# First product-key layer computed densely for both token tiles, with the first tile's chain behind it

## The chip, the core and the metric

The kernel runs on one core of one Trainium2 chip. The metric is device time in microseconds (us), from the start of the program on the core to its end. All arithmetic that matters here is float32. The engines are named as in the profile: PE is TensorE (matmuls), PEld its weight loads, DVE is VectorE, ACT is ScalarE, POOL is GpSimd (which here issues the gathers), SP is SyncE (which here issues all other loads).

## The reference, cut to what matters

One batch of 256 tokens with 1,024 features passes through a first block (token mixing, attention, 32 experts) and then a second block of two layers. The change touches the feed-forward part of the second block's first layer, a product-key memory:

```python
def peer_ffn(h, w_q, sub_keys, u_tab, v_tab):       # T = 256 tokens, D = 1024
    q = (xt @ w_q).reshape(T, PEER_HEADS, 2, PEER_HALF)         # 8 heads
    s = jnp.einsum('thpd,hpnd->thpn', q, sub_keys)              # 2 x 128 key scores
    sv, si = lax.top_k(s, PEER_TOPK)                            # 16 of 128
    cand = sv[:, :, 0, :, None] + sv[:, :, 1, None, :]
    cv, ci = lax.top_k(cand.reshape(T, 8, 256), PEER_TOPK)      # 16 of 256 pairs
    ...
    eidx = (i1 * PEER_NKEYS + i2)                               # row of 16,384
    gates = jax.nn.softmax(cv, axis=-1)
    uc = jnp.take(u_tab, ic, axis=0); vc = jnp.take(v_tab, ic, axis=0)
    act = jax.nn.gelu(jnp.einsum('cd,ckd->ck', xc, uc))
    return jnp.einsum('ck,ckd->cd', gc * act, vc)
```

A token uses 8 x 16 = 128 of the 16,384 rows of `u_tab` and of `v_tab` (64 MiB each). After it follow a gated embedding, and then in the second layer keys and values, stick-breaking attention, and a second product-key memory with tables of its own.

## The kernel before

The tokens are two tiles of 128. Up to the recurrent part everything is dense. Then come four phases of 128 steps, `f` = 0 to 3 (`PHASES`): phases 0 and 1 are the first memory for tile 0 and tile 1, phases 2 and 3 the second memory for tile 0 and tile 1. A step `k` handles one pick of each of the 128 tokens:

- POOL gathers 128 rows of 8 KiB (key and value side by side, `uv0` or `uv1`) into one of 10, later 13, row buffers: 1 MiB a step.
- DVE (`share`, line 2170) multiplies each row by its token and sums; ACT takes the gelu (1664 or 1662) of a pair of steps; DVE multiplies by the gate (2199 or 2196); ACT spreads each coefficient on a diagonal (1669).
- PE (`picks`, 1245) multiplies the diagonal by the value rows and adds into two banks: two matmuls of 512 columns a step.

A phase has 64 ticks of two steps. In a tick `t` of phase `f` >= 1, a piece of `chain(f - 1, t)` is issued behind the picks on each engine. `chain(q)` is all that follows a memory for a tile: `chain(0)` and `chain(1)` are the embedding of the first layer, keys, values, queries, attention in four groups of heads, output product, and the queries and scores of the second memory; `chain(2)` and `chain(3)` are only the last embedding and norm. So `chain(0)` runs under phase 1, `chain(1)` under phase 2.

The choice of rows is DVE's: a unit is one head of one tile (`UNITS` = 16 in a layer), cut in four pieces, `best_keys` twice, `best_pairs`, `rows_of` (lines 2104 to 2150). A list of ticks (`FIRST_CHOICES`, `chosen`) sets where a piece stands between the shares. A gather waits for the unit's numbers (`idx_ready`) and for a free row buffer (`rows_used`, counted by PE).

The weights of a chain, 60 chunks of 512 KiB, are loaded by SP into a ring of 6 slots in the order in which the chain uses them; earlier loads use a ring of 8. SP waits for a slot's last use (`w_used`) before it refills it.

Of the kernel before, what the change touches and what calls it, by code (L numbers as in the profile page):

```python
# [31 lines left out]
P = 128  # L32
T = 256
# [29 lines left out]
ROWS, MORE_ROWS, MORE_AT = 10, 3, 170  # L63
ROW = 2 * D
UNITS = TT * PH
# [24 lines left out]
FIRST_NEXT, ASK_HERE, ASK_NEXT = 0, 11, 19  # L90
FIRST_CHOICES = {0: (1, 2), 1: (1, 3), 2: (2, 0), 4: (2, 1), 6: (2, 2), 8: (2, 3), 10: (3, 0), 12: (3, 1), 14: (3, 2),
# [3 lines left out]
QUERY_GROUPS = (range(0, 4), range(4, 8))  # L95
EARLY = 10
PLE_EARLY = 5

# [35 lines left out]
def plan():  # L134

    first, n = {}, 0
    for name, chunks in (
        ("w_in", 16), ("w_pool", 1), ("w_out", 8), ("w_router", 1), ("b_down", 1), ("proj0", 2), ("ple0", 8),
        ("a_x", 8), ("a_y", 8),
        ("wqa", 8), ("wqb", 8),  # L140
        *((f"{name}{q}", chunks) for q in range(TT) for name, chunks in (
            ("proj_", 2), ("ple_", 8), ("kv", 16 - EARLY * (q == 0)), ("bq", 8), ("bo", 8),
# [15 lines left out]

def row_buffer(k):

    return k % ROWS if k < MORE_AT else (k - MORE_AT + ROWS) % (ROWS + MORE_ROWS)


ROW_COUNT = []
for _k in range(PHASES * PHASE):
    ROW_COUNT.append(sum(row_buffer(m) == row_buffer(_k) for m in range(_k + 1)))


def chosen(f, t):

    if f == 0:
        return [FIRST_CHOICES[t]] if t in FIRST_CHOICES else []
    now = [(PH * f + 2 + j // 4, j % 4) for j in range(24) if int(1.75 * j) == t]
    if f < PHASES - 1 and CHOOSE <= t < CHOOSE + 8:
        now.append((PH * (f + 1) + (t - CHOOSE) // 4, (t - CHOOSE) % 4))
    return now


def by_tanh(f, t):

    return 1 <= f <= TT and t // SHARES in TANH_UNITS
# [29 lines left out]
def program(nc, io, out):  # L211
    first = plan()
    slot, slot_loads, freed_by = ring_plan(first)
    with ExitStack() as ctx:
# [36 lines left out]
        def half(bank, e):  # L251
# [19 lines left out]
            "pq_ready scores_kept tok_ready idx_ready cv_ready cv_exp dots_ready gelu_ready coef_ready "  # L271
            "diags_ready rows_used x_turned x_kept xk_ready rms_kept hs_ready h_turned hd_act hd_dve gate_kept "
            "k_copied k_turned k2_ready v2_ready q_copied q_turned q2_ready "
            "z_done ln_ready spm_ready rc_done arg_ready w_exp a_ready o_done o_ready tile_done scored sq_tile ss_tile rt_tile gates_done sums_in sq_summed root_turned col_ready early_used late_used "
            "out_ready out_stored moe_step gu_used dn_used"
# [3 lines left out]
        keys_loaded, gates_loaded = sem("keys_loaded"), sem("gates_loaded")  # L279
        early_loaded, late_loaded = sem("early_loaded"), sem("late_loaded")  # L280
# [65 lines left out]
        early = [at(k * D, D) for k in (0, 1, 2, 3, 6, 7, 8, 9, 10, 11)]  # L346
# [6 lines left out]
        sums_bank = (7, 6, 4, 6, 0, 1, 7, 4)  # L353
# [12 lines left out]
        def asked(z, tt):  # L366

            return scr if z else (big[:, 5 * ROW:5 * ROW + D], mT[:, D:2 * D])[tt]

        def ask_bank(z, tt):  # L370

            return ((4, 4), (4, 0))[z][tt]

        def score_bank(z, tt):

            return ((0, 4), (4, 0))[z][tt]
# [14 lines left out]
        diag_at = small[:, 2304:2304 + DIAGS * P]  # L391

# [54 lines left out]
        def _(sync):  # L447
# [107 lines left out]
            for z in range(2):  # L555
                sync.dma_start(keys0[z], io["sub_keys"][0][:, z * SLOT:(z + 1) * SLOT]).then_inc(keys_loaded, 16)
            for k in range(EARLY):
                c, z = k % DT, k // DT
                sync.dma_start(early[k], io["w_kv"][c * P:(c + 1) * P, z * SLOT:(z + 1) * SLOT]).then_inc(early_loaded, 16)
            dense("wqa", io["peer_w_q"][0], 2)  # L560

            def ple_chain(q):
                if q == 0:
                    sync.wait_ge(w_used, first["proj0"] + 2)
# [1846 lines left out]
```

## Time and profile before

| what | us |
|---|---|
| measured, median of 3 runs (lowest, highest) | 2735.54 (2732.45, 2740.74) |
| profiled execution, span from first to last instruction | 2730.7 |
| PE busy | 2497.4 |
| DVE busy | 1372.8 |
| ACT busy | 626.5 |
| POOL busy | 494.7 |
| bytes moved | 1058.03 MB, mean 387 GB/s |

The profile gives no time of its own for the profiled execution beyond this span; the median of the runs is 4.8 us above it, which is what lies around the span. Busy PE time is the union of pipelined matmuls, so for groups of matmuls of one kind the busy time divided by their count is the interval from one to the next. An "x8" row of the timeline is eight instructions merged.

### The profile page before, as it was taken

Reading aid. Unit: us, or ns where it says so; the run is one execution under the profiler, and the core shown is the slowest. Engines: PE = TensorE matmul, PEld = TensorE weight load, DVE = VectorE, ACT = ScalarE, POOL = GpSimd, SP = SyncE. Lnnn points to the kernel's source line nnn. Section 1 sums busy time; section 2 is a strip of 40 time slices with the busy share of each in tenths; the row PEclk is TensorE's granted clock in tenths of the full one; section 3 lists DMA queues with packets and bytes.
Section 4 is the critical chain, followed back from the end, with each engine's and each line's share of the span. In section 5 each row is a group of like instructions: output and inputs, shape, how many; then the busy total and the mean of one; then the engine's idle time right before and its main releaser. Section 6 shows DMA issues by size and latency. Waiting matters only on the chain.

```text
span 2730.7 us, 30447 instructions
## 1 busy us (share of the span) xinstructions
PE 2497.4 (91%) x10712; PEld 1284.3 (47%) x10712; DVE 1372.8 (50%) x3805; ACT 626.5 (23%) x1464; POOL 494.7 (18%) x534
## 2 busy tenths in 40 slices
PE   8899999999999999997987889989799899788786
PEld 6744444444444444995643334436344446333332
DVE  2411222222212222757677776785675775678753
ACT  0300110100100001232322342332332432332212
POOL 1000000000000000003333333332332332333330
PEclk9989999999999999998999999999999999999999
DMA  7689999999999997549999999999999999999993
GB/s 250 262 325 409 429 428 429 428 428 428 428 429 427 430 427 296 183 170 381 421 420 421 421 419 383 419 420 418 420 418 417 420 418 417 417 411 421 421 421 165
DMA packets 135686, 1058.03 MB, mean 387 GB/s; under 512 B 15744, under 2 KB 16168, under 8 KB 45472
## 3 DMA queue, kind: packets, MB, share of 16 engines
q0 software_dynamic: 75104, 540.07, 47.9%
q1 hardware_dynamic: 60480, 516.70, 45.8%
q8 instruction: 52, 0.85, 0.1%
q14 instruction: 50, 0.41, 0.0%
HBM read 1055.64 MB, written 2.63 MB: 388 GB/s over the span
## 4 chain that ended last, share of the span: by engine, by line
PE 55%; DMA 28%; DVE 12%; ACT 3%; issue 2%; SPq 0%; DVEq 0%; POOL 0%; POOLq 0%
PE ps L773 15%; PE ps L1245 15%; DMA big<-in_uv,small 14%; DMA big<-in_w_gate_up 13%; PE ps L763 4%; PE ps L927 4%; DVE big L2170 4%; PE ps L1042 2%; PE ps L1198 2%; PE ps L1058 2%; PE ps L809 1%; PE ps L623 1%; PE ps L695 1%; DMA ring<-in_uv,small 1%; PE ps L1005 1%
## 5 line engine op out<-in xcount | busy, mean ns | idle before, releaser
L1245 PE MATMUL ps<-big,small 128*128 128x512 f32 x1940 | 922.5, 622 | 171.1 <-ACT small L1669 170.9
L2342 POOL DMA_INDIRECT big<-in_uv,small x485 | 458.9, 946 | 2086.6 <-DVE small L2150 1182.7
L773 PE MATMUL ps<-big 128*64 128x512 f32 x3072 | 701.7, 601 | 11.6 <-DMA big<-in_w_gate_up 7.7
L2170 DVE SCALAR_TENSOR_TENSOR big<-big,ps 128x1024 f32<-128x1024 f32 x485 | 580.8, 1217 | 213.9 <-DMA big<-in_uv,small 213.6
L1245 PEld LDWEIGHTS ps<-big,small 128*128 128x128 f32 x1940 | 371.7, 199 | 662.1 <-issue 410.7
L773 PEld LDWEIGHTS ps<-big 128*64 128x64 f32 x3072 | 205.5, 137 | 397.7 <-issue 355.4
L1669 ACT ACTIVATE small<-con,small 128x128 f32<-128x128 f32 x512 | 177.6, 394 | 322.4 <-DVE small L2199 273.2
L1908 DVE COPY big<-ps 128x512 f32<-128x512 f32 x32 | 22.1, 692 | 417.5 <-PE ps L773 417.5
L1894 DVE TENSOR_TENSOR big<-ps,big 128x256 f32<-128x256 f32 x64 | 27.2, 425 | 284.7 <-PE ps L791 284.7
L1664 ACT ACTIVATE small<-small 128x2 f32<-128x2 f32 x224 | 45.7, 204 | 495.1 <-DVE big L2170 479.1
L927 PEld LDWEIGHTS ps<-hT,ring 128*128 128x128 f32 x1152 | 134.5, 194 | 14.7 <-issue 10.5
L927 PE MATMUL ps<-hT,ring 128*128 128x128 f32 x1152 | 135.6, 278 | 3.7 <-DVE hT L1968 3.7
L763 PEld LDWEIGHTS ps<-small,mT 128*128 128x128 f32 x1024 | 120.0, 196 | 26.6 <-issue 26.6
L763 PE MATMUL ps<-small,mT 128*128 128x64 f32 x1024 | 124.4, 281 | 1.3 <-DVE small L1876 1.3
L1421 ACT COPY big<-ps 128x512 f32<-128x512 f32 x32 | 18.7, 585 | 412.9 <-PE ps L773 412.9
L2199 DVE SCALAR_TENSOR_TENSOR small<-small 128x2 f32<-128x2 f32 x224 | 49.2, 220 | 124.3 <-ACT small L1664 122.8
L1413 ACT ACTIVATE big<-big 128x256 f32<-128x256 f32 x64 | 26.6, 416 | 218.2 <-DVE big L1895 218.2
L1042 PE MATMUL ps<-ring,xT 128*128 128x512 f32 x152 | 68.3, 593 | 0.0
L1245 PE MATMUL ps<-ring,small 128*128 128x512 f32 x108 | 54.9, 634 | 13.0 <-ACT small L1669 13.0
L809 PE MATMUL ps<-small,big 64*128 64x256 f32 x512 | 63.9, 390 | 0.0
L1198 PEld LDWEIGHTS ps<-xT,ring 128*128 128x128 f32 x512 | 59.5, 192 | 6.7 <-issue 6.7
L1401 ACT COPY big<-ps 128x512 f32<-128x512 f32 x32 | 18.7, 586 | 184.3 <-PE ps L773 184.3
(338 smaller groups left out, 2104.8 us busy)
## 6 DMA issues: line engine op xcount, KB each, us to landing
big<-in_w_gate_up SPq DMA_DIRECT2D x128, 2048.0 KB, 21.0
big<-in_w_down SPq DMA_DIRECT2D x64, 2048.0 KB, 22.4
ring<-in_peer_w_q SPq DMA_DIRECT2D x48, 512.0 KB, 10.7
ring<-in_ple_w_gate SPq DMA_DIRECT2D x22, 512.0 KB, 10.5
ring<-in_w_kv SPq DMA_DIRECT2D x22, 512.0 KB, 10.4
ring<-in_w_in SPq DMA_DIRECT2D x16, 512.0 KB, 7.1
ring<-in_a_w_in SPq DMA_DIRECT2D x16, 512.0 KB, 4.7
ring<-in_b_w_q SPq DMA_DIRECT2D x16, 512.0 KB, 11.7
```

Source lines behind the costliest of these rows:

```text
L763: last = pe.matmul(ps[:, G_X, c * CAP:(c + 1) * CAP], mT[:, tt * D + c * P:tt * D + (c + 1) * P], m_sel[:, tt * CAP:(tt + 1) * CAP], start ...
L773: last = pe.matmul(ps[side * CAP:(side + 1) * CAP, bank + b, :], o, w[:, at:at + BANK], start=start, stop=stop, skip_group_check=True)
L809: last = pe.matmul(half(G_OUT, side * DT // 2 + c), m_y[at, c * P:(c + 1) * P], m_gateT[at, :], start=False, stop=True, skip_group_check=True)
L927: last = pe.matmul(ps[:, bank + e // 4, (e % 4) * P:(e % 4 + 1) * P], w[:, e * P:(e + 1) * P], src(c)[:, tt * P:(tt + 1) * P], start=(c == ...
L1042: last = pe.matmul(ps[:, bank + z, :], src[:, blocks(c)], w[:, z * BANK:(z + 1) * BANK], start=(c == 0), stop=(c == DT - 1), skip_group_ch ...
L1058: last = pe.matmul(ps[:, bank + half_, :], src[:, blocks(c)], w[:, half_ * BANK:(half_ + 1) * BANK], start=(c == 0), stop=(c == DT - 1), s ...
L1198: last = pe.matmul(ps[:, A + e // 4, blocks(e % 4)], w[:, blocks(e)], hd[:, blocks(c)], start=(c == 0 and e % 4 == 0), stop=(c == DT - 1), ...
L1245: last = pe.matmul(ps[:, out_bank(f) + z, :], diagonal(k), rows(k)[:, D + z * BANK:D + (z + 1) * BANK], start=(k % PHASE == 0), stop=((k + ...
L1669: act.activation(diagonal(k), ident, ACT.Copy, scale=coef[:, k % PICKS:k % PICKS + 1])\
L2170: ins = dve.scalar_tensor_tensor(r, r, 1.0, tok, op0=ALU.mult, op1=ALU.mult, accum_out=dots[:, k % PICKS:k % PICKS + 1])
L2199: dve.scalar_tensor_tensor(coef[:, at], acts[:, at], p_rec[:, u16:u16 + 1], cv[:, at], op0=ALU.mult, op1=ALU.mult).then_inc(S["coef_ready" ...
L2342: pool.indirect_dma_start(out=rows(k), out_offset=None, in_=io[f"uv{n // UNITS}"], in_offset=bass.IndirectOffsetOnAxis(ap=rows_at[:, at:at ...
```

## The change

Phases 0 and 1 are replaced. Instead of gathering the chosen rows, the kernel streams all of both tables once, and computes every key's score for every token of both tiles:

- `key_block`: for each of 128 blocks (one second-key number, 128 first-key numbers) one chunk of 512 KiB is loaded into the ring of 8 and multiplied by all 256 tokens: 8 matmuls of 256 columns. `keep_keys` on ACT takes the gelu of two blocks at a time into `weighed`, 128 KiB per partition that cover all of `big`.
- `choose`: all 16 units are chosen without shares between them; the row number is not formed, the two key numbers and the scores are kept. `gates` makes the softmax weights, `turn_picks` transposes numbers and gates to have a token's 128 picks on the partitions.
- `place`, 64 times: for 8 tokens and 64 second keys, DVE builds one-hot rows of the first keys (`hot`, 1,024 wide) and gate-weighted one-hot rows of the second keys (two operations of 512), PE multiplies them token by token (8 matmuls of 64 columns, the sum over a token's 128 picks), and DVE multiplies `weighed` by the outcome (`weigh`, 512 wide, from PSUM). 32 of them stand between the later key blocks, 32 between the first 63 value blocks.
- `value_block`: for each of 128 blocks a chunk of 512 KiB is multiplied by `weighed`: 4 matmuls of 512 columns, two tiles by two halves.
- `chain(0)` is issued alone after the last value block, then phase 2 with `chain(1)` and phase 3 with `chain(2)` as before. The second memory's gathers begin with unit 16, which is chosen at ticks 51 to 54 of that lone chain; all 13 row buffers are free by then. The ten early key and value weights of `chain(0)` are now loaded by the ring; the second half of the first queries' weights takes their place.

```diff
+            def key_block(k):
+                w, bank = chunk(first["u"] + k), KEY_BANK + k // 2 % 2
+                if k % 2 == 0 and k >= 4:
+                    pe.wait_ge(S["keys_kept"], k - 2)
+                for c in range(DT):
+                    done = pe.matmul(ps[:, bank, k % 2 * T:(k % 2 + 1) * T], w[:, c * P:(c + 1) * P], tile(hT, c), ...)
+                done.then_inc(w_used, 1)
+            def place(b):
+                tt, t0, tokens, lo, n = placing(b)
+                pe.wait_ge(S["hot_ready"], b + 2)
+                if b == 32:
+                    pe.wait_ge(S["keys_kept"], BLOCKS)
+                if b >= 2:
+                    pe.wait_ge(S["w_ready"], b - 1)
+                for j in range(tokens):
+                    done = pe.matmul(..., hot1[b % 2][:, j * P:(j + 1) * P], hot2[b % 2][:, j * n:(j + 1) * n], ...)
+                done.then_inc(S["placed"], 1)
+            def value_block(k):
+                if k in PLACED_BY:
+                    pe.wait_ge(S["w_ready"], PLACED_BY[k])
+                w = chunk(first["v"] + k)
+                for tt in range(TT):
+                    for z in range(2):
+                        done = pe.matmul(ps[:, out_bank(tt) + z, :], weighed[tt][:, k * P:(k + 1) * P], w[:, z * BANK:(z + 1) * BANK], ...)
+                done.then_inc(w_used, 1)
+            pe.wait_ge(S["idx_ready"], PH // 2)
+            for k in range(BLOCKS):
+                key_block(k)
...
+            for k in range(BLOCKS):
+                value_block(k)
...
+            for t in range(TICKS):
+                chain(0, t)
-            for f in range(1, PHASES):
+            for f in range(TT, PHASES):
...
+            def keep_keys(j):
+                used_through(act, "u", 2 * j + 2)
+                for tt in range(TT):
+                    act.activation(at, sums[:, :, tt * P:(tt + 1) * P], ACT.Gelu_apprx_tanh).then_inc(S["keys_kept"], 1)
+            for j in range(BLOCKS // 2):
+                keep_keys(j)
+                if j in EXPS_AT:
+                    exps(EXPS_AT[j])
...
+            def hot(b):
+                dve.tensor_tensor(one, iota..., of(0)..., ALU.is_equal)
+                link(dve.tensor_tensor(two, iota[:, lo:lo + n]..., of(1)..., ALU.is_equal))
+                dve.tensor_tensor(two, two, of(2)..., ALU.mult).then_inc(S["hot_ready"], 1)
+            def weigh(b):
+                dve.wait_ge(S["placed"], b + 2)
+                dve.wait_ge(S["keys_kept"], lo + n)
+                dve.tensor_tensor(w, ps[:, PLACE_BANK[b // 32] + b % 2, :].rearrange("p (t i) -> p i t", t=tokens), w, ALU.mult)
+            for b in range(PLACINGS):
+                weigh(b)
+                if b + 2 < PLACINGS:
+                    hot(b + 2)
-            for n in range(2 * UNITS):
+            for n in range(UNITS, 2 * UNITS):
                 pool.wait_ge(S["idx_ready"], n + 1)
```

`EXPS_AT` puts the exponentials of unit `n` behind key pair `5 * (n - 3) // 2 + 1`, `PICKS_AT` puts `turn_picks` behind pair 36, and `PLACE_IN_KEYS` spreads 32 placings over pairs 37 to 62.

Three places in the order of instructions. PE, from the end of the recurrent output product, before (L927 is `one_tile`, here the queries of tile 1, and L1245 the picks):

```order
L1005 MATMUL ps<-mT,big 128x128 x24
L1227 MATMUL ps<-con,hT 128x128 x8
L942 MATMUL ps<-small,con 128x128
L927 MATMUL ps<-hT,ring 128x128 x8
L1245 MATMUL ps<-big,small 128x512 x4
...
L1245 MATMUL ps<-big,small 128x512 x8
L1219 MATMUL ps<-big,mT 128x128 x8
```

And now (L1252 is `second_queries`, L1269 `key_block`, L1278 `turn_picks`, L1290 `place`):

```order
L1026 MATMUL ps<-mT,big 128x128 x24
L1252 MATMUL ps<-hT,big 128x128 x32
L963 MATMUL ps<-small,con 128x128
...
L1234 MATMUL ps<-big,mT 128x128 x8
L1269 MATMUL ps<-hT,ring 128x256 x16
L1234 MATMUL ps<-big 128x128 x8
L1269 MATMUL ps<-hT,ring 128x256 x576
L1278 MATMUL ps<-con,small 128x128 x6
L1269 MATMUL ps<-hT,ring 128x256 x16
L1290 MATMUL ps<-small,mT 128x64 x16
```

The queries that stood between picks are now issued in one piece, and 74 key blocks (16 + 576 matmuls, 8 a block) stand before `turn_picks`; from there one or two placings stand behind each pair of blocks.

PE in `chain(0)`, at its gate and keys, before (L1058 is keys and values, L1065 a transposition):

```order
L1058 MATMUL ps<-ring,xT 128x512 x4
L1245 MATMUL ps<-big,small 128x512 x4
L1042 MATMUL ps<-ring,xT 128x512 x4
L1245 MATMUL ps<-big,small 128x512 x4
L1042 MATMUL ps<-ring,xT 128x512 x4
```

And the same chain now, from the last value blocks (L1301) on (L1063 is L1042 of before, L1073 is L1058, L1080 is L1065, L1165 the attention scores):

```order
L1301 MATMUL ps<-ring,big 128x512 x260
L1099 MATMUL ps<-ring,pT 128x512 x4
L1080 MATMUL ps<-con,big 128x128 x8
L1063 MATMUL ps<-ring,xT 128x512 x16
L1080 MATMUL ps<-con,big 128x128 x8
L1073 MATMUL ps<-ring,xT 128x512 x24
L1080 MATMUL ps<-con,big 128x128 x8
L1073 MATMUL ps<-ring,xT 128x512 x8
L1063 MATMUL ps<-ring,xT 128x512 x16
L1080 MATMUL ps<-con,big 128x128 x8
L1165 MATMUL ps<-xT,big 128x128 x4
```

The picks between the chain's pieces are gone; nothing else stands between them. DVE, from the last unit of the first memory to the first placings, now (L2222 ends `rows_of`, L2384 and L2386 are `gates`, L2390 takes the turned picks, L2400 to L2404 are `hot`, L2412 is `weigh`):

```order
L2222 TENSOR_REDUCE small<-small 128x16
L2384 RECIPROCAL small<-small 128x16
L2386 TENSOR_TENSOR small<-small 128x256
L2390 COPY small<-ps 128x3x128 x2
L2400 TENSOR_TENSOR mT<-con,small 128x1024
L2402 TENSOR_TENSOR small<-con,small 128x512
L2404 TENSOR_TENSOR small<-small 128x512
L2400 TENSOR_TENSOR mT<-con,small 128x1024
L2402 TENSOR_TENSOR small<-con,small 128x512
L2404 TENSOR_TENSOR small<-small 128x512
L2412 TENSOR_TENSOR big<-ps,big 128x64x8
```

Before, a pair of `share` operations of 1,024 elements stood between any two pieces of a unit; now units 2 to 15 follow each other directly behind the norm of the second tile, and the placings come after the last of them.

## Rows read from the trace of the kernel before

**Rows 1.** The page: span, busy us of each engine, GB/s in 40 slices.
```profile
span 2730.7 us, 30447 instructions
PE 2497.4 (91%) x10712; PEld 1284.3 (47%) x10712; DVE 1372.8 (50%) x3805; ACT 626.5 (23%) x1464; POOL 494.7 (18%) x534
...
GB/s 250 262 325 409 429 428 429 428 428 428 428 429 427 430 427 296 183 170 381 421 420 421 421 419 383 419 420 418 420 418 417 420 418 417 417 411 421 421 421 165
```

**Rows 2.** Phases: stretch, PE PEld DVE ACT POOL busy (count), PEclk, DMA share, GB/s.
```profile
1244.00:1586.00 342.00, 297.18 (x968) 155.43 (x968) 250.33 (x676) 91.13 (x243) 120.53 (x128) 0.93 1.01 420
1586.00:1984.00 398.00, 358.30 (x1112) 176.68 (x1112) 275.70 (x760) 132.41 (x311) 127.34 (x134) 0.98 1.01 413
1984.00:2387.00 403.00, 361.61 (x1186) 183.27 (x1185) 267.98 (x728) 131.75 (x297) 119.86 (x127) 0.97 1.02 418
2387.00:2700.00 313.00, 256.04 (x553) 104.34 (x552) 220.28 (x553) 83.66 (x225) 107.61 (x114) 0.96 0.97 403
```

**Rows 3.** Who waited for whom, 1244 to 2700: us, times, longest.
```profile
DVE big L2170 <- DMA big<-in_uv,small: 213.6, 169, 3.5
```

**Rows 4.** Timeline, PE: start, duration, instructions of one kind in a row.
```profile
19.93 20.99 PE L623 MATMUL ps<-hT,ring 128*128 128x256 f32 x96
...
1211.64 9.20 PE L1257 MATMUL ps<-hT,ring 128*128 128x128 f32 x80
...
1705.44 3.60 PE L1042 MATMUL ps<-ring,xT 128*128 128x512 f32 x8
```

**Rows 5.** Timeline, DVE: the first unit's pieces, and the first share.
```profile
1221.77 0.30 DVE L2104 MAX8 small<-ps 128x8 f32<-128x128 f32 x1 [8.35 <-PE ps L1267]
...
1225.21 0.18 DVE L2126 CAST small<-small 128x32 f32<-128x32 uint32 x1
...
1228.20 0.17 DVE L2140 TENSOR_SCALAR small<-small 128x16 uint32<-128x16 uint32 x1
...
1231.77 0.17 DVE L2148 SCALAR_TENSOR_TENSOR small<-small 128x16 f32<-128x16 f32 x1
...
1243.79 1.22 DVE L2170 SCALAR_TENSOR_TENSOR big<-big,ps 128x1024 f32<-128x1024 f32 x1
```

**Rows 6.** Groups by line and shape: busy, mean ns of one, idle before.
```profile
L1957 DVE TENSOR_REDUCE small<-mT 128x128 f32<-128x1024 f32 x4 | 7.6, 1912 | 1.4 <-ACT mT L1459 1.4
L2249 DVE TENSOR_TENSOR big<-ps,big 128x512 f32<-128x512 f32 x8 | 5.5, 685 | 10.6 <-ACT big L1551 10.6
```

**Rows 7.** Bytes by queue, 1984 to 2700.
```profile
q0 software_dynamic: 35611, 259.28, 87.3%
q1 hardware_dynamic: 9792, 34.87, 12.2%
```

**Rows 8.** Timeline, the last rows and the last chain, engines together.
```profile
2699.19 1.22 DVE L2170 SCALAR_TENSOR_TENSOR big<-big,ps 128x1024 f32<-128x1024 f32 x1 [1.23 <-DMA big<-in_uv,small]
...
2705.21 1.29 DVE L2215 TENSOR_TENSOR hT<-ps,hT 128x512 f32<-128x512 f32 x2 [4.30 <-PE ps L1245]
...
2708.70 1.07 ACT L1528 ACTIVATE big<-hT 128x1024 f32<-128x1024 f32 x1
...
2711.17 0.29 ACT L1529 ACTIVATE small<-small,eps 128x1 f32<-128x1 f32 x1
```

**Rows 9.** Timeline, ACT: the logarithm of a group of heads in `chain(0)`.
```profile
1742.41 1.28 ACT L1601 ACT_TABLE_LOAD   x1
1743.70 0.63 ACT L1601 ACTIVATE big<-big 128x512 f32<-128x512 f32 x1
```

**Rows 10.** Loads of 512 KiB: median us to landing; busy and GB/s at 60:100.
```profile
ring<-in_w_out SPq DMA_DIRECT2D x8, 512.0 KB, 3.8
...
big<-in_w_kv SPq DMA_DIRECT2D x10, 512.0 KB, 11.7
...
60.00:100.00 40.00, 37.64 (x183) 27.02 (x182) 17.76 (x58) 17.23 (x52) 0.00 (x0) 1.00 0.86 349
```

**Rows 11.** Busy and clock where PE resumes after waiting.
```profile
1244.00:1248.00 4.00, 3.72 (x16) 3.42 (x16) 3.90 (x12) 0.20 (x1) 0.69 (x1) 0.50 1.02 426
```

More of the change, by code:

```diff
@@ L570, in _ @@
[L570 to L582 removed]
+                sync.dma_start(keys0[z], io["sub_keys"][0][:, z * SLOT:(z + 1) * SLOT]).then_inc(gates_loaded, 16)
@@ L583, in _ @@
+            for t in range(TICKS):
+                chain_weights(0, t)
+            for t in range(TICKS):
+                chain_weights(1, t)
             sync.wait_ge(w_used, first["proj_1"] + 2)
@@ L1236, in residual, with second_queries @@
                 for c in range(DT):
-                    last = pe.transpose(ps[:, 4 + c // 4, (c % 4) * P:(c % 4 + 1) * P],
-                                        tile(xT, c)[:, tt * P:(tt + 1) * P], ident)
-                last.then_inc(S["x_turned"], 1)
+                    done = pe.transpose(narrow(TURN_BANK, c), tile(xT, c)[:, tt * P:(tt + 1) * P], ident)
+                done.then_inc(S["x_turned"], 1)
+            def second_queries(tt, between=()):
+                pe.wait_ge(early_loaded, 16 * DT)
+                for c in range(DT):
+                    for e in range(DT):
+                        done = pe.matmul(narrow(ask_bank(1, tt), e), wqb[c][:, e * P:(e + 1) * P],
+                                         tile(hT, c)[:, tt * P:(tt + 1) * P], start=(c == 0 and e % 4 == 0),
+                                         stop=(c == DT - 1), skip_group_check=True)
+                    if tt:
+                        done.then_inc(S["early_used"], 1)
+                    elif c == DT - 1:
+                        done.then_inc(S["tile_done"], 1)
+                    for after, piece in between:
+                        if c == after:
+                            piece()
@@ new lines, in key_block @@
+            def key_block(k):
+                w, bank = chunk(first["u"] + k), KEY_BANK + k // 2 % 2
+                if k % 2 == 0 and k >= 4:
+                    pe.wait_ge(S["keys_kept"], k - 2)
+                for c in range(DT):
+                    done = pe.matmul(ps[:, bank, k % 2 * T:(k % 2 + 1) * T], w[:, c * P:(c + 1) * P], tile(hT, c),
+                                     start=(c == 0 and k % 2 == 0), stop=(c == DT - 1), skip_group_check=True)
+                done.then_inc(w_used, 1)
@@ new lines, in _ @@
+            pe.wait_ge(S["idx_ready"], PH // 2)
+            for k in range(BLOCKS):
+                key_block(k)
+                if k == 1:
+                    scores(1, 1)
+                if k % 2:
+                    if k // 2 == PICKS_AT:
+                        turn_picks()
+                    for b in PLACE_IN_KEYS[k // 2]:
+                        place(b)
+            for k in range(BLOCKS):
+                value_block(k)
+                if k in RESIDUAL_AT:
+                    residual(RESIDUAL_AT[k])
+                if k in PLACE_IN_VALUES:
+                    place(PLACE_IN_VALUES[k])
```

356 lines of the change are left out of this document (191 added, 165 removed), and 3 rows, old and new, of the table FIRST_CHOICES.

## The prediction

> **What bounds the kernel now.** I read the busy time by stage first. From 1244 to 2700 us, the four phases, the 16 DMA engines are busy 97 to 102% of the time and move 403 to 420 GB/s, whatever else goes on [rows 2]. PE is busy 82 to 90% there, DVE 66 to 73%. The page alone would mislead: over the span PE has the larger share, 91% [rows 1], but its records overlap and part of that busy time is at a lower granted clock (0.93 in phase 0). The waits decide it: the dot products on DVE waited 213.6 us in 169 pieces for gathered rows [rows 3], and those rows could not come faster. So phases 0 to 3 last as long as their bytes: 1.05 MB a step, 134.2 MB a phase, plus the chain's weights. Phases 0 and 1 take 1984 - 1244 = 740 us [rows 2], and they hold the whole of `chain(0)` as free cover for PE, ACT and DVE.
>
> **The change, part by part.** I follow absolute times in the profiled execution, up to the last share's first gather, then add what comes behind.
>
> *Start of the key blocks.* PE's first key block waits for four finished units. A unit is on DVE from 1221.77 to 1231.77 plus two short operations [rows 5]: keys 3.4 us, pairs 3.0, rows 3.6 without these two, which fall away: 10.0 us. At 1243.8 the second tile's norm is done and unit 1 has its keys [rows 5]. Left are 6.6 us of unit 1 and units 2 and 3, 20 us: the blocks start at 1270.4. PE has 128 + 64 query matmuls of 128 columns until then, 0.115 us each (9.20/80) [rows 4], 22 us, so it waits for DVE, not DVE for it.
>
> *Key blocks.* 1,024 matmuls of 256 columns. An unbroken run of such matmuls takes 20.99 us for 96, less the pipe's end of 0.35: 0.215 us each [rows 4]. That is 220.2 us. The load of a block is 0.524 MB in 1.72 us, 305 GB/s, below what the queue shows (next paragraph but one). DVE must meanwhile finish units 4 to 15: 12 x 10.0 = 120 us, and PE reaches `turn_picks` after 37 pairs, 127 us. ACT's exponential of unit 15 stands behind pair 31 (at 111 us) and its pair scores come at 116; ACT then holds back the gelus, and PE, two banks ahead, loses 1 to 2 us.
>
> *Placings.* 512 matmuls of 64 columns. No such matmul stands alone before; I take the interval of a 128-column one, 0.11 us, since its weights are as wide: 57 us for all 64 placings, on PE and not hidden. As DVE work a placing costs 1.2 us (1,024 elements, as the share's 1.22 [rows 5]) and three times 0.69 (512 elements [rows 6]), with overlap 3.2 us. PE offers one per 3.69 us during keys (26 x 3.44 / 32 + 0.9) and one per 4.4 during values, so DVE fits. First wait: two `hot` of 2.6 us after the picks are turned, about 2 us beyond a pair.
> The price of `weigh` is the open one: it reads PSUM and walks `weighed` with strides. A reduction that reads 1,024 strided elements takes 1.91 us [rows 6], 1.87 ns an element against 1.34 for the plain 512. Bounds: 0.69 us, or 0.96, and as a far end twice that, 1.9. At 0.96 a placing is 3.5 us and still fits. At 1.9 it is 4.4, PE waits 0.7 us in each of 32 placings in the keys and none in the values: +22 us. I take nothing.
> The Trainium skill (SBUF — State Buffer, "Door 1: The DMA port swizzle") says that each access that crosses to a new 16-byte line pays a penalty, and that any non-contiguous PSUM pattern significantly slows matmuls. The strided reduction agrees in direction (1.91 us); no row here shows a strided PSUM read, and if it tripled `weigh` the 22 us above would be due.
>
> *Value blocks.* 512 matmuls of 512 columns at 0.429 us (3.60/8 with 0.17 of pipe end [rows 4]): 219.7 us. The transposes of picks and residual are 22 small ones, 2.5 us. I add 8 us: ACT 1.5, first placing 2, and PE's wait before the blocks and after the turn, since PE comes back at a granted clock of 0.50, 1.2 GHz, after waiting [rows 11].
> End of the values: 1270.4 + 220.2 + 57.3 + 219.7 + 2.5 + 8 = 1778.
>
> *Are the loads hidden?* 134.2 MB in 508 us are 264 GB/s, 305 at the peak. 512 KiB loads: ten in a row landed after 11.7 us in the median, and with larger ones between, 349 GB/s were moved while PE was the one that asked [rows 10]. Alone such a load lands in 3.8 us [rows 10]; eight in flight would be 8 x 0.524 / 3.8 = 1,100 GB/s, more than the engines have. So the ring of 8 hides them.
> The Trainium skill (DMA: Bandwidth & Descriptors, "Measured (HBM→SBUF, 128 partitions, SWDGE, issued from GpSimd)") asks for at least 1 MiB a DMA for 75% of peak; by it the change halves the size to where less is had. Its table is for one DMA at a time. The case of 349 GB/s above is against it.
>
> *`chain(0)` alone.* Before, it had 398 us of cover; now each step counts. From rows of the last chain [rows 8]: add 1.3, turn and gains 2.3, square to root 2708.70 to 2711.46 = 2.8, reciprocal and scale 0.9. Steps to the embedding's gate 7.5; its 16 matmuls 7.3; sigmoid with table load and the two products 4.1; square, scale, turn, eight gains 7.2; keys and values 32 x 0.43 = 13.7, but ten of their chunks come at 1.25 us (0.524 MB at 420 GB/s [rows 2]), so 16; the queries likewise 8 x 1.25 = 10; copy, turn, keep 4. Four groups of heads: from ln to ln a group passes DVE twice 0.69, PE sums and the next scores 1.5, abs, exp, exp and ln at 0.63 each [rows 9] and some 0.7 of handing over, 6.1 us; a table load of 1.28 on the first [rows 9], and 12 us for the first half of the first and the second half of the last: 30. Merge 5.6, add to gains 7.5, first queries 7.2 and their copy, scores and keep 3.6, unit 16 10.3. Sum 120. PE waits often here, so part of its 65 us of matmuls (84 of 512 columns at 0.43, 128 of 128 at 0.115, some 14 us of transposes, scores and attention) runs at 1.2 GHz as in [rows 11]; I take 10 us for it (bounds: 0, and 65 if all of it). First gather: 1778 + 130 = 1908.
>
> *Phases 2 and 3.* They stay bound by bytes. From 1984 to 2700 SP's queue moved 34.9 MB [rows 7], the same work as now. The gathers are all 256: 268.4 MB instead of the 259.3 counted there, since none can be ahead of the lone chain. 303.3 MB at phase 2's 418 GB/s [rows 2] are 725.6 us; 1.5 for the first to arrive. Behind the last row, 2699.2 to 2730.7, are 31.5 us [rows 1, 8]. End: 1908 + 1.5 + 725.6 + 31.5 = 2667 us, 64 less than the span of 2730.7. The median of the runs lies 4.8 above that span: 2672.
>
> In bytes: 268 MB of gathers for the first layer become 134 MB of streams, which saves 320 us of DMA; about 260 of them are given back, since PE's 497 us of new matmuls and 130 us of chain have no bytes beneath them.
>
> **The rivals.**
> A. *The lone chain is slower than summed* (half clock nearly throughout, loads later, handing over dearer): its bound of 65 us instead of 10 adds 55, end at 2727. For it: PE resumed at 0.50 [rows 11] and attention has many waits. Against: gate, keys to queries, and merge to scores are runs of 7 us and more. With half of it, 2700.
> B. *DVE sets the pace of the placings*: +22 us in the keys, 2694; if `hot` with its broadcasts is also dearer, by a third (+1 us), +32 more in keys and +32 in values, 2758. For it: no row has this broadcast at this width. Against: the share of 1,024 elements takes 1.22 us with one operand in PSUM [rows 5], so the width alone costs nothing more.
> C. *The streams are bound by DMA: slower than before.* At the 250 GB/s of the span's first slice [rows 1], whose loads are of this size, 134.2 MB take 537 us instead of 508, +29: 2701. It decides from 134.2 MB / (508 + 64) = 235 GB/s down; at the 170 of the weakest slice before the phases [rows 1], 789 us and 2953. Against: 349 GB/s [rows 10], and that those slices stand where PE does not ask for more.
> D. *The chain is quicker and PE never waits*: 120 for the chain, 3 instead of 8: 2657.
> That the change doesn't do what it says I leave out: the order of PE shows both streams and the lone chain.
>
> **How the numbers follow.** Forecast with D's side, 2650 to 2692: 0.62. A, 2692 to 2727: 0.18. B: 0.12, of which 0.03 above 2744. C: 0.05, of which 0.03 slower. Faster still, below 2650: 0.03. A measurement of this kernel tells 0.3%, 8.2 us: same is 2727 to 2744. Faster 0.89, same 0.05, slower 0.06. The range leaves out a tenth or less at each end: 2648 to 2716.
>
> **What would show it.** Right: PE busy near 100% from 1270 to 1778 at clock 1.00, matmuls of 256 columns at 0.215 us and of 512 at 0.43, DMA near 270 GB/s; PE waiting for DVE before the first key block; the first gather 125 to 135 us after the last value block; then 418 GB/s for 725 us. Wrong: PE waiting for `in_u_blocks` or `in_v_blocks` (C), for the products on L2404 or L2412 with DVE near 100% (B), a chain of 160 us or more (A), or a second memory that starts below 418 GB/s, because DVE chooses unit 17 before its first share while 13 buffers fill.

## The result, and the profile after

| | us, median | lowest to highest |
|---|---|---|
| before | 2735.2 (4 runs) | 2732.45 to 2740.74 |
| after | 3229.03 (4 runs) | 3227.3 to 3231.69 |

The changed kernel is 18% slower: ratio 1.181, 95% interval 1.1793 to 1.1827. The forecast said 2672 us. The profiled execution has a span of 3227.1 us; by the forecast's own sum it should have been 2667.

The page of the changed kernel, against [rows 1]: the busy time of each engine, GB/s in 40 slices, and the engines of the chain that ended last.

```profile
span 3227.1 us, 35837 instructions
PE 3033.2 (94%) x13774; PEld 1789.1 (55%) x13774; DVE 1235.1 (38%) x3327; ACT 548.3 (17%) x1202; POOL 253.8 (8%) x278
...
GB/s 257 231 407 428 428 428 428 429 429 429 429 429 428 215 187 66 150 151 155 119 118 115 120 123 118 137 151 149 184 129 318 418 419 420 418 419 417 421 421 218
...
PE 72%; DMA 16%; DVE 8%; ACT 3%; issue 1%; another core or an unknown queue 0%; SPq 0%; DVEq 0%; POOL 0%; POOLq 0%
```

PE went from 2497.4 us busy to 3033.2, 536 more, and the wide trough of 115 to 184 GB/s in the middle is the dense stage. The stretches (columns as in [rows 2]) are keys, values, the lone chain, and the second layer's gathers:

```profile
1270.00:1781.00 511.00, 511.00 (x2669) 458.11 (x2668) 215.31 (x583) 84.54 (x185) 0.00 (x0) 1.00 0.39 131
1781.00:2280.00 499.00, 498.82 (x1555) 253.43 (x1553) 94.95 (x123) 2.81 (x6) 0.00 (x0) 1.00 0.39 132
2280.00:2455.00 175.00, 130.58 (x539) 80.26 (x540) 34.49 (x89) 44.11 (x72) 0.01 (x1) 0.83 0.51 172
...
2484.00:2886.00 402.00, 368.33 (x1193) 186.01 (x1192) 271.05 (x739) 134.17 (x303) 121.48 (x128) 0.96 1.02 418
2886.00:3196.00 310.00, 255.13 (x554) 103.88 (x552) 218.17 (x545) 81.61 (x221) 108.30 (x114) 0.97 0.98 408
```

For 1,010 us PE is busy without a gap (but 0.2 us) at full clock, with the DMA engines at 39%. Only from the second layer's gathers on is the picture that of [rows 2] again. The groups of the new lines give the reason (L1269 is `key_block`, L1301 `value_block`, L1290 `place`, L2400 to L2404 the one-hot tiles, L2412 `weigh`):

```profile
L1269 PE MATMUL ps<-hT,ring 128*128 128x256 f32 x2048 | 448.2, 380 | 0.0
L1301 PE MATMUL ps<-ring,big 128*128 128x512 f32 x1024 | 446.6, 594 | 0.0
...
L1290 PE MATMUL ps<-small,mT 128*128 128x64 f32 x1024 | 120.6, 272 | 0.0
L2400 DVE TENSOR_TENSOR mT<-con,small 128x1024 f32<-128x1024 f32 x64 | 77.8, 1215 | 0.0
L2404 DVE TENSOR_TENSOR small<-small 128x512 f32<-128x512 f32 x64 | 44.3, 692 | 2.2
L2412 DVE TENSOR_TENSOR big<-ps,big 128x512 f32<-128x512 f32 x64 | 44.2, 691 | 317.2 <-PE ps L1290 317.2
```

The program has 128 blocks x 8 = 1,024 key products, 128 x 4 = 512 value products and 64 x 8 = 512 placing products. The trace has 2,048, 1,024 and 1,024. **Each of these float32 products stands in the trace as two records, one behind the other.** Their busy times add to 1,015 us where the forecast counted 497. (They add to a little more than the 1,000.3 us from the first key product to the end of the values, because the pipelined ends of one group overlap the next.) The start of the keys shows it at the smallest size; between the first two blocks (16 products) and the rest stand only second scores:

```profile
1279.63 7.07 PE L1269 MATMUL ps<-hT,ring 128*128 128x256 f32 x32
1286.54 1.95 PE L1234 MATMUL ps<-big 128*128 128x128 f32 x16
1288.32 42.04 PE L1269 MATMUL ps<-hT,ring 128*128 128x256 f32 x194
```

Not every float32 instruction on PE is doubled: the transposes, which the program issues on PE as well, have one record each. `turn_picks` has 6 in the program and 6 in the trace, and the next product starts 0.66 us after the first of them, 0.11 us for each:

```profile
1536.96 0.82 PE L1278 MATMUL ps<-con,small 128*128 128x128 f32 x6
1537.62 7.07 PE L1269 MATMUL ps<-hT,ring 128*128 128x256 f32 x32
```

The doubling was to be seen before the change. Phases 0 to 3 of the kernel before have 512 steps of `share` with two products each, 1,024 in all; its trace counts 1940 + 108 = 2,048 for them:

```profile
L1245 PE MATMUL ps<-big,small 128*128 128x512 f32 x1940 | 922.5, 622 | 171.1 <-ACT small L1669 170.9
...
L1245 PE MATMUL ps<-ring,small 128*128 128x512 f32 x108 | 54.9, 634 | 13.0 <-ACT small L1669 13.0
```

The signs that the forecast named for its rivals B and C did not show: no wait of PE for `in_u_blocks` or `in_v_blocks`, none of PE for DVE in the dense stage. Rival A's sign, a chain of 160 us or more, did: it took 175. The long waits of the dense stage are waits for PE but for one, the gates' wait for the exponentials (L1716), which stand on ACT between gelus that wait for PE themselves (us in total, times, longest):

```profile
ACT big L1725 <- PE ps L1269: 416.4, 64, 9.8
DVE big L2412 <- PE ps L1290: 317.2, 58, 12.4
...
DVE hT L2296 <- PE ps L1301: 222.6, 1, 222.6
DVE small L2384 <- ACT small L1716: 116.5, 1, 116.5
```

### The profile page after: what moved, and what is told of

Read it like the earlier page. It is cut to its first block, busy times and chain, and to the rows that moved or that the text cites. A ratio compares the mean times of both kernels' runs of the same rounds, so it can differ in the third digit from the quotient of the medians.

```text
span 3227.1 us, 35837 instructions
## 1 busy us (share of the span) xinstructions
PE 3033.2 (94%) x13774; PEld 1789.1 (55%) x13774; DVE 1235.1 (38%) x3327; ACT 548.3 (17%) x1202; POOL 253.8 (8%) x278
## 4 chain that ended last, share of the span: by engine, by line
PE 72%; DMA 16%; DVE 8%; ACT 3%; issue 1%; another core or an unknown queue 0%; SPq 0%; DVEq 0%; POOL 0%; POOLq 0%
PE ps L1269 14%; PE ps L1301 14%; PE ps L794 14%; DMA big<-in_w_gate_up 9%; DMA big<-in_uv,small 6%; PE ps L1310 5%; PE ps L784 4%; PE ps L1290 3%; PE ps L948 3%; PE ps L1063 2%; DVE big L2251 2%; PE ps L1073 2%; PE ps L1213 1%; PE ps L830 1%; PE ps L644 1%
## 5 line engine op out<-in xcount | busy, mean ns | idle before, releaser
L794 PE MATMUL ps<-big 128*64 128x512 f32 x3072 | 700.3, 600 | 10.6 <-DMA big<-in_w_gate_up 6.8
L1310 PE MATMUL ps<-big,small 128*128 128x512 f32 x944 | 455.1, 628 | 103.3 <-ACT small L1741 103.2
L1269 PE MATMUL ps<-hT,ring 128*128 128x256 f32 x2048 | 448.2, 380 | 0.0
L2468 POOL DMA_INDIRECT big<-in_uv,small x236 | 224.4, 951 | 2838.4 <-DVE small L2231 2401.8
L1301 PE MATMUL ps<-ring,big 128*128 128x512 f32 x1024 | 446.6, 594 | 0.0
L794 PEld LDWEIGHTS ps<-big 128*64 128x64 f32 x3072 | 205.4, 137 | 395.9 <-issue 357.2
L1269 PEld LDWEIGHTS ps<-hT,ring 128*128 128x128 f32 x2048 | 386.9, 190 | 51.4
L1310 PEld LDWEIGHTS ps<-big,small 128*128 128x128 f32 x944 | 181.8, 200 | 353.9 <-issue 218.5
L1301 PEld LDWEIGHTS ps<-ring,big 128*128 128x128 f32 x1024 | 192.1, 190 | 229.2 <-issue 229.1
L2251 DVE SCALAR_TENSOR_TENSOR big<-big,ps 128x1024 f32<-128x1024 f32 x236 | 281.4, 1216 | 76.9 <-DMA big<-in_uv,small 68.0
L2412 DVE TENSOR_TENSOR big<-ps,big 128x512 f32<-128x512 f32 x64 | 44.2, 691 | 317.2 <-PE ps L1290 317.2
L784 PEld LDWEIGHTS ps<-small,mT 128*128 128x128 f32 x1024 | 120.0, 196 | 26.6 <-issue 26.6
L1290 PEld LDWEIGHTS ps<-small,mT 128*128 128x128 f32 x1024 | 123.3, 192 | 15.7 <-issue 14.3
L784 PE MATMUL ps<-small,mT 128*128 128x64 f32 x1024 | 124.4, 281 | 1.3 <-DVE small L1949 1.3
L1290 PE MATMUL ps<-small,mT 128*128 128x64 f32 x1024 | 120.6, 272 | 0.0
L948 PEld LDWEIGHTS ps<-hT,ring 128*128 128x128 f32 x896 | 100.7, 192 | 0.2 <-DVE hT L2041 0.2
```

The source lines that it names most:

```text
L784: last = pe.matmul(ps[:, G_X, c * CAP:(c + 1) * CAP], mT[:, tt * D + c * P:tt * D + (c + 1) * P], m_sel[:, tt * CAP:(tt + 1) * CAP], start ...
L794: last = pe.matmul(ps[side * CAP:(side + 1) * CAP, bank + b, :], o, w[:, at:at + BANK], start=start, stop=stop, skip_group_check=True)
L948: last = pe.matmul(ps[:, bank + e // 4, (e % 4) * P:(e % 4 + 1) * P], w[:, e * P:(e + 1) * P], src(c)[:, tt * P:(tt + 1) * P], start=(c == ...
L1269: done = pe.matmul(ps[:, bank, k % 2 * T:(k % 2 + 1) * T], w[:, c * P:(c + 1) * P], tile(hT, c), start=(c == 0 and k % 2 == 0), stop=(c == ...
L1290: done = pe.matmul(ps[:, PLACE_BANK[b // 32] + b % 2, j * n:(j + 1) * n], hot1[b % 2][:, j * P:(j + 1) * P], hot2[b % 2][:, j * n:(j + 1) ...
L1301: done = pe.matmul(ps[:, out_bank(tt) + z, :], weighed[tt][:, k * P:(k + 1) * P], w[:, z * BANK:(z + 1) * BANK], start=(k == 0), stop=(k = ...
```

## The experiments

From the first `add` of `chain(0)` to the end of the span, the changed kernel takes 3227.1 - 2279.9 = 947.2 us. Where a run below changes the dense stage, I give the time of that `add`, since it splits the span at the end of the values. Runs without a range are single ones. The diffs are cut to the lines that matter.

### One tile's products, all loads

```diff
 # key_block                                        # value_block
-...tile(hT, c)                                     -for tt in range(TT):
+...tile(hT, c)[:, 0:P]                             +for tt in range(1):
```

> The changed kernel with the key and value products of the first product-key layer for the first tile alone: every block of keys and values is still loaded and the other engines' instructions stay, but TensorE multiplies a key block with 128 tokens instead of 256 and a value block into one tile's sums instead of two. Left out: the first layer's result for the second tile. Theory (TensorE bounds the dense stage, because a float32 product costs two records of the trace): 2,048 key records of 0.11 instead of 0.215 us and 512 value records instead of 1,024 take away about 225 + 220 = 445 us of matrix work; of the keys' part some is given back, since VectorE's choosing and its placings (about 15 x 10 + 2 x 32 x 2.6 us) then last as long: 2,800 to 2,900 us. Rival (the streams, the ring of eight buffers or the loads bound the stage, TensorE waits hidden in its records): 3,180 to 3,240 us.

Measured 2797.9 us, 431 less than 3229.0. The `add` stands at 1849.8, 430 earlier. TensorE's work bounds the stage; the rival is out. The groups:

```profile
L1269 PE MATMUL ps<-hT,ring 128*128 128x128 f32 x2048 | 234.8, 276 | 0.0
...
L1301 PE MATMUL ps<-ring,big 128*128 128x512 f32 x512 | 226.9, 596 | 0.0
```

With 128 columns instead of 256 the key records fall from 448.2 to 234.8 us; still two for each product. The two groups lost 433 us together, and the run is 431 us shorter. The same bytes now came in 568 us instead of 1,000, and PE still waited for no block; the first row is the whole stage, the second its end, behind the last placing:

```profile
1281.50:1849.80 568.30, 567.59 (x3624) 444.37 (x3622) 301.05 (x670) 86.26 (x189) 0.00 (x0) 1.00 0.69 233
...
1738.00:1849.80 111.80, 111.68 (x261) 49.15 (x260) 0.70 (x2) 0.00 (x0) 0.00 (x0) 1.00 0.83 285
```

That the time came out 2 us under what I expected is because VectorE did not hold the keys up: PE waited 0.6 us for its one-hot tiles.

### The same products, small loads

```diff
-load(first["u"] + k, io["u_blocks"][k, :, :])
+load(first["u"] + k, io["u_blocks"][k, :, 0:64], cols=64)      # the values alike
```

> The changed kernel, but each of the 256 loads of a key or value block brings 64 of its 1,024 columns; TensorE multiplies the same number of columns (what lies in the rest of the buffer is old). Left out: most of the first layer's keys and values. Theory (TensorE bounds the dense stage by its own work): 3,215 to 3,235 us, no change, although 126 MB fewer are moved. Rival (the streams bound it, as the forecast's third rival had it): well below 3,100 us.

Measured 3237.4 us, one run. The DMA share of the dense stretches fell from 0.39 to 0.04, and nothing was gained:

```profile
1270.00:1781.00 511.00, 511.00 (x2699) 458.90 (x2698) 219.95 (x610) 85.27 (x187) 0.00 (x0) 1.00 0.04 9
1781.00:2280.00 499.00, 499.00 (x1583) 257.76 (x1582) 97.96 (x126) 3.46 (x8) 0.00 (x0) 1.00 0.04 10
```

So the forecast's third rival, a stage bound by its streams, is out as well. The run is 8 us longer than the changed kernel, but the stage is not: its `add` stands at 2288.5 and its first key product at 1288.18, 1,000.3 us apart, as in the changed kernel (1279.63 to 2279.93). The 8.6 us were lost ahead of the edited part, 8 of them before the first product of L794 (150.7 us against 142.7), where the granted clock was 0.57 from 120 to 140 us and 0.66 from 140 to 160, against 0.87 and 0.79. Why it differed there is open.

### Placings of one token in eight

```diff
-for j in range(tokens):
+for j in range(1):
     done = pe.matmul(ps[:, PLACE_BANK[b // 32] + b % 2, j * n:(j + 1) * n], ...
```

> The changed kernel with one of the eight tokens of each placing multiplied: 64 products instead of 512; VectorE still builds all one-hot tiles and weighs all 64 times. Left out: the gates of seven tokens in eight. Theory (TensorE's work alone sets the stage, 1,024 records of placings take 120.6 us): 3,229 - 105 = about 3,124 us. Rival (VectorE's one-hot tiles and weighings pace the placings, as the forecast's second rival had it): less than 40 us gone, 3,190 us or more.

Measured 3128.6 us, 100.5 less; 105 were expected. From the first key product (1280.30) to the `add` (2180.6) are 900.3 us instead of 1,000.3. The placings cost what their records on PE say, and VectorE, which still did all of its part, paces nothing here.

### The kernel before, half of its picks' products

```diff
 def picks(f, t):
-    for z in range(2):
+    for z in range(1):
         last = pe.matmul(ps[:, out_bank(f) + z, :], diagonal(k), ...
```

> The kernel before with half the matrix work of the picked rows: each row is multiplied into one half of the output (one bank of 512 columns) instead of two, in all four phases; the gathers, VectorE's products and ScalarE's diagonals stay. Left out: half the output columns of both product-key layers. Reading in the forecast (the gathers' 151 MB a phase bound the kernel before, TensorE's work lies beneath): 2,720 to 2,740 us, no change. Rival (TensorE's doubled records bound the kernel before as well): about 110 us less for each phase, 2,300 to 2,400 us.

Measured 2737.1 us beside 2731.8 for the kernel before in the same job: no gain from half the work. PE's busy time and DMA share by phase (phases 0 to 2):

```profile
1244.00:1586.00 342.00, 219.06 (x708) 118.10 (x709) 248.92 (x672) 90.10 (x239) 121.13 (x129) 0.81 1.01 420
1586.00:1984.00 398.00, 285.75 (x853) 137.90 (x852) 277.46 (x767) 132.82 (x315) 128.36 (x137) 0.87 1.02 419
1984.00:2387.00 403.00, 292.00 (x932) 145.24 (x930) 268.32 (x724) 130.05 (x295) 118.44 (x127) 0.86 1.01 415
```

In these three phases PE fell from between 87 and 90% busy [rows 2] to between 64 and 73%, and about as many gathers are issued in each (129, 136 and 127 against 128, 137 and 127). That reading of the kernel before was right: bytes bound it. PE's busy time fell by less than its work, because the granted clock fell as well, from 0.93 to 0.98 [rows 2] to between 0.81 and 0.87. The kernel before was also nearer to its second bound than the forecast's count of products made it look: the first 342 us had 297 us of PE [rows 2].

### The lone chain with half of its dense columns

```diff
 # stationary and key_value, in chain(0) alone
-ps[:, bank + z, :], src[:, blocks(c)], w[:, z * BANK:(z + 1) * BANK]
+ps[:, bank + z, 0:n_], src[:, blocks(c)], w[:, z * BANK:z * BANK + n_]      # n_ = 256
```

> The changed kernel with the lone chain's dense products halved: in chain(0) alone the gate, keys and values, queries and merge multiply 256 of each 512 columns, all their weights are loaded as before. Left out: half of those products' columns for the first tile. From the changed kernel's trace the lone chain takes 175 us from the add to the first gather, 45 more than forecast, and PE is busy 131 us of it where the forecast counted 65. Theory (the chain is longer because each float32 product costs two records): 160 records of 0.43 us become 160 of 0.215, 34 us less, less what the chunks (32 of 0.524 MB at about 1.25 us, of which some are there before) then hold back: the first gather 20 to 34 us earlier after the add, total 3,195 to 3,210. Rival (waits, half clock and handing over make it longer, the chunks set the pace of the products): under 10 us less, 3,220 to 3,235.

Measured 3205.5 us, 23.6 less. From the `add` at 2280.2 to the first gather at 2431.8 are 151.6 us, where the changed kernel has 175.1 (2279.93 to 2454.99). The expectation took 34 us from the products, 160 records at full clock. By the groups their busy time fell from 72.7 us (29.3 + 27.9 + 15.5) to 42.8 (17.4 + 16.4 + 9.0), 29.9 less, and the idle time before them rose from 3.6 to 8.9 us, 4.5 of it for chunks, for which the changed kernel does not wait here. That leaves 24.6; 23.5 show up. Two of the three groups:

```profile
L1075 PE MATMUL ps<-ring,xT 128*128 128x256 f32 x64 | 17.4, 418 | 4.7 <-ACT xT L1605 2.3 <-DMA ring<-in_w_kv 2.2
L1064 PE MATMUL ps<-ring,xT 128*128 128x256 f32 x64 | 16.4, 394 | 4.2 <-DMA ring<-in_b_w_q 1.9 <-ACT xT L1605 1.3 <-DMA ring<-in_ple_w_gate 0.4
```

### Bfloat16 in the key and value products

```diff
+weighed = tuple(big[:, a:a + BLOCKS * P // 2].bitcast(BF16) for a in (BLOCKS * P, 0))
+hTb = big[:, 30720:31744].bitcast(BF16)                          # ACT copies hT here
-load(first["u"] + k, io["u_blocks"][k, :, :])                    # SyncE; the values alike
+pool.dma_start(ring[:, slot[m], 0:SLOT // 2].bitcast(BF16), io["u_blocks"][k, :, :])
```

> The changed kernel with bfloat16 operands in the key and value products alone: the 256 blocks are loaded on GpSimd's queue, which converts them on the way in, ScalarE copies hT to bfloat16 (four copies) and writes its gelus as bfloat16, VectorE's weighings too; sums stay float32, the placings' products stay float32. Changed: the first product-key layer's operands are rounded to bfloat16. Theory (a float32 product costs two records at two cycles a column, so bfloat16 costs a quarter): 1,024 key products in 1,024 records of about 0.107 us = 110 us, 512 value products of about 0.216 = 110 us, placings 121 us as before; 1,010 us of TensorE work become 340, and the stage then ends with the last of VectorE (141 us of choosing, 64 x 3.3 us of placings, to about 1,620) and the streams (134 MB at 350 GB/s: about 1,665): the values end at 1,640 to 1,730 instead of 2,280, total 2,560 to 2,700, under the kernel before. Rival (the two records are bookkeeping of the trace, the time per column is that of any product): values end near 2,280 and the total near 3,230. Second rival (the loads on GpSimd's queue, 3 us and more one after the other, pace the stage): values end at 2,050 or later, total 3,000.

Measured 2643.0 us (2640.5 to 2652.7, 4 runs): 0.9676 of the kernel before, interval 0.9648 to 0.9703, and 586 us under the changed kernel. The `add` stands at 1691.2. The groups:

```profile
L1273 PE MATMUL ps<-big,ring 128*128 128x256 bf16 x1024 | 132.8, 289 | 32.5 <-ACT big L1729 29.5 <-DMA ring<-in_u_blocks 2.9
...
L1305 PE MATMUL ps<-ring,big 128*128 128x512 bf16 x512 | 125.4, 380 | 12.4 <-DMA ring<-in_v_blocks 12.4
...
L1294 PE MATMUL ps<-small,mT 128*128 128x64 f32 x1024 | 122.6, 274 | 2.4 <-DVE small L2412 2.4
```

The bfloat16 products have one record each, the float32 placings beside them, in the same kernel, still two. And where the two alternate without a gap, the time of one can be read from the starts:

```profile
1480.46 1.91 PE L1273 MATMUL ps<-big,ring 128*128 128x256 bf16 x16
1482.20 3.68 PE L1294 MATMUL ps<-small,mT 128*128 128x64 f32 x32
1485.72 1.91 PE L1273 MATMUL ps<-big,ring 128*128 128x256 bf16 x16
```

Sixteen bfloat16 products of 256 columns take 1482.20 - 1480.46 = 1.74 us, 0.109 each. In float32 the first sixteen took 1286.54 - 1279.63 = 6.91 us, 0.432 each: four times as much. So each of the two float32 records, 0.216 us, takes as long as two bfloat16 products. Sixteen placing products of float32 (32 records) take 3.52 us, 0.22 each, and they have only 64 columns.

The Trainium skill (FP8 and Floating Point Precision, "TensorE Precision Notes") says that true float32 takes four passes through the array. The two measured times, 0.432 and 0.109 us, agree with four; the passes themselves are not to be seen, and the trace shows two records for a product. This rule was not weighed in the forecast.

The conversion is done by the DMA on GpSimd's queue. The Trainium skill (DMA: Bandwidth & Descriptors, "SWDGE vs HWDGE vs iDMA") says that only that queue can do it. It did not become a bound: GpSimd needed 0.53 us for each. In the last stretch a block's four products start every 1.25 us, 0.524 MB read in 1.25 us or 419 GB/s (the profile counts such a load as 256 KiB, as written, and gives 214 GB/s from 1632 to 1690, at a DMA share of 1.12). PE waits for each block there, so the streams themselves are the limit:

```profile
1630.60 1.04 PE L1305 MATMUL ps<-ring,big 128*128 128x512 bf16 x4 [0.21 <-DMA ring<-in_v_blocks]
1631.85 1.04 PE L1305 MATMUL ps<-ring,big 128*128 128x512 bf16 x4 [0.22 <-DMA ring<-in_v_blocks]
```

### Bfloat16 in the placings too

```diff
-hot1 = [mT[:, k * D:(k + 1) * D] for k in range(2)]
+hot1 = [mT[:, k * D:(k + 1) * D - D // 2].bitcast(BF16) for k in range(2)]      # hot2 alike
```

> As the kernel with bfloat16 streams, and the one-hot tiles of the placings written as bfloat16 too (so the gates are rounded to bfloat16 before they are placed). Theory: 512 products of placings in 512 records, 30 to 60 us of TensorE work instead of 121, VectorE's three instructions of a placing unchanged or shorter; if TensorE or VectorE still bounds some of the stage, 20 to 90 us less than with bfloat16 streams alone; if the streams bound it, within 10 us of it.

Measured 2617.4 us (2616.3 to 2619.0, 4 runs): 0.9569 of the kernel before, interval 0.955 to 0.9587, 118 us less, and 25.7 less than with bfloat16 streams alone, where 20 to 90 were expected. This is the fastest version in this study that computes everything, at the price of bfloat16 rounding in the first layer.

```profile
L2408 DVE TENSOR_TENSOR mT<-con,small 128x1024 bf16<-128x1024 f32 x64 | 77.8, 1215 | 0.0
...
L1294 PE MATMUL ps<-small,mT 128*128 128x64 bf16 x512 | 27.5, 199 | 56.6 <-DVE small L2412 56.5
```

PE's placings fell from 122.6 to 27.5 us, but now PE waits 56.5 us for the one-hot tiles: the forecast's second rival, VectorE as the pace of the placings, comes true only here. Its instructions did not get shorter with the narrower output (1,215 ns as in float32).

### The same with small loads

```diff
+n = SLOT if m < first["u"] + RING else 64
-pool.dma_start(ring[:, slot[m], 0:SLOT // 2].bitcast(BF16), io[f"{seg}_blocks"][k, :, :])
+pool.dma_start(ring[:, slot[m], 0:n // 2].bitcast(BF16), io[f"{seg}_blocks"][k, :, 0:n])
```

> As the kernel with bfloat16 streams and placings, but only the first eight blocks of keys are loaded whole, and each of the 248 later loads brings 64 of its 1,024 columns; TensorE, VectorE and ScalarE do the same work. Left out: most of the first layer's keys and values. It tells what bounds the stage that bfloat16 left (1,280 to 1,670). Theory A (the streams: the DMA engines' share is 0.86 to 1.03 there, TensorE waited 52 us for value blocks): values end some 50 us earlier or more, total 2,560 or less. Theory B (VectorE's choosing and placings, 64 x 3.3 us, which end near 1,600, with the values behind them): total 2,595 to 2,617.

Measured 2593.9 us, 23.5 less than with whole loads; the `add` stands at 1645.4 instead of 1670.5. That is 1 us below theory B's range and far from A's: the streams cost the last 25 us, while the one-hot tiles and weighings (to 1589) hold the stage before them. TensorE is the limit only at the end: from 1589 to 1645 it is busy throughout with the value blocks that needed the last placings.

```profile
1278.00:1589.00 311.00, 217.10 (x1822) 149.34 (x1821) 294.35 (x665) 84.37 (x189) 100.78 (x191) 0.91 0.17 11
1589.00:1645.00 56.00, 56.00 (x264) 25.15 (x260) 0.85 (x2) 0.00 (x0) 30.07 (x57) 1.00 0.31 29
```

The columns are those of [rows 2]; in the first stretch DVE is busy 294 of 311 us.

## Why the prediction was wrong

**The step that failed** is the pricing of the new products: "1,024 matmuls of 256 columns ... 0.215 us each", "57 us for all 64 placings", "512 matmuls of 512 columns at 0.429 us". The prices were per record of the trace, the counts per matmul of the program, and a float32 matmul has two records. The same slip stands in the lone chain's count. In the dense stage none of the rivals that I named took place, and the range was wrong because every case in it had the same wrong count. The runs put the cost of a float32 product at 0.432 us for 256 columns where 0.215 was taken.

| step | forecast | measured |
|---|---|---|
| keys begin | 1270.4, PE waits for DVE | 1279.6, PE without a gap |
| key products | 220.2 | 448.2 |
| placings | 57 | 120.6 |
| value products | 219.7 | 446.6 |
| end of the values | 1778 | 2279.9 |
| lone chain | 130 | 175.1 |
| first gather to the end | 758.6 | 772.1 |

The last three are 502, 45 and 13.5 us too short, 560.5 together; the span is 560.1 above the forecast's 2667, which was 2666.6 before rounding. The three groups of products are busy times that overlap a little at their edges, so the start and the groups add to 2,295 and not to 2279.9. The 4.8 us that were added for what lies around the span were too many: the profiled run took 3228.86 us with its span of 3227.1, 1.8 more.

- *Start of the keys.* The queries were undercounted as well: 192 products at 0.115 us were to leave PE waiting, but each is two records (second queries, L1252: 256 records for 128 products), and PE is at work without a gap until the keys, 9 us after the time forecast for DVE. DVE's part was right: it is done with the fourth unit at 1270.3, forecast 1270.4.
- *Placings beside DVE.* `weigh`, the open price, took 0.691 us, its low bound. The rule of the Trainium skill that I set against it (SBUF — State Buffer, "Door 1: The DMA port swizzle") was not felt: reading PSUM in steps of 64 elements, VectorE took 0.691 us, against 0.685 for contiguous ones. It is a weak test of that rule, since what the Trainium skill says of PSUM there is on matmuls, and in SBUF `weigh` finds eight elements side by side. The one-hot tiles took 1.215, 0.685 and 0.692 as forecast. Rival B was out before it began: with PE's doubled products the 64 weighings stand 8 us apart (1546.5 to 2056.6).
- *Loads.* Hidden, as said, but at 132 GB/s instead of 264, so the claim was hardly tested by the changed kernel. The one-tile run tested it better: 233 GB/s over the stage, 285 over its last 112 us, and no wait for a block. The bfloat16 run is a harder case on another queue: there PE waited 12.4 us for value blocks and 2.9 for key blocks.
- *The lone chain.* The forecast has 65 us of products, the trace 130.6 us of PE. The shortened chain took 29.9 us of these away and got 23.5 us of the 45 back. Another 10 us stand in the first queries, which no run changed: 64 products, 128 records, take 17.17 us where the forecast had 7.2. At full clock 128 such records take 14.46 us, so some 7 us are the doubling and some 3 a lower clock. By this estimate 31 of the 45 us are doubled records. The other 12 or so were not measured apart; half clock is among them: in the attention stretch the granted clock was 0.54, PE 17.6 us busy in 40.

```profile
2422.84 17.17 PE L1213 MATMUL ps<-xT,ring 128*128 128x128 f32 x128 [1.27 <-ACT xT L1603]
...
2443.06 14.46 PE L1213 MATMUL ps<-xT,ring 128*128 128x128 f32 x128
...
2360.00:2400.00 40.00, 17.64 (x74) 11.56 (x75) 10.38 (x15) 22.20 (x28) 0.00 (x0) 0.54 0.01 3
```

- *Phases 2 and 3.* 741 us from 2455 to 3196 at a mean of 413 GB/s, where I took 727.1 at 418: the first 29 us ran at 401, below the 418 that the forecast wanted there, and the last phase at 408. A matter of size only.
- *Which side is the bound.* For the kernel before, bytes: shown by the run with half the picks. The error was to conclude from it that PE had room. For one tile dense, float32 work on PE is 235 us of keys and 227 of values in the one-tile run and half of the 121 of placings, 522 us together, against 134.2 MB / 418 GB/s = 321 us of gathers (both are estimates). In bfloat16 keys and values of both tiles together were 132.8 + 125.4 us of PE.

## What to carry to other kernels

Before pricing new work by a row of the trace, divide that row's count by the number of such instructions that the program issues: here 2,048 records for 1,024 matmuls, visible in the profile of before, would have added 497 us for the new products and up to 65 for the lone chain, and 2672 us would have become 3,170 to 3,235, an estimate from the forecast's own terms. Only the products count double in this trace, the transposes do not. Trading bytes for products needs the spare time of the engine that takes them over, product by product and in the type in which they run: in float32 this change loses 18%, with bfloat16 operands the same structure gains 4.3%. When a resource is freed by a factor of four, look at once for the next bound: with bfloat16, VectorE's one-hot tiles and the streams stood within 25 us of each other.

## What the hardware showed beyond that

- A float32 product of 64 columns with 128x128 weights costs PE 0.22 us (3.52 us for 16), in two records 0.11 apart, half of what 256 columns cost. In bfloat16 eight of them before the next product start within 0.23 us (0.03 each):

```profile
1500.30 0.40 PE L1294 MATMUL ps<-small,mT 128*128 128x64 bf16 x8
1500.53 1.89 PE L1305 MATMUL ps<-ring,big 128*128 128x512 bf16 x8
```

- A float32 transpose of 128 columns on PE took 0.11 us and has one record (6 in 0.66 us); a float32 product of 128 columns took 0.23 us in two records (1,024 in 234.8 us, the one-tile run).
- VectorE's comparison of 1,024 elements with a broadcast operand took 1,215 ns whether it wrote float32 or bfloat16. The product of 512 with the gates took 692 ns with the tile that it reads and writes in either type; the gates stay float32.
- GpSimd spent 528 ns on each of the 256 converting loads, which read 134 MB at up to 419 GB/s (from the bytes that the program reads).
